# Turning the residual on VectorE, and three more up-projection units by [hi|lo] products, in a two-block transformer kernel

## What is computed

```python
    x = x + merged @ w_o
    h2 = rmsnorm(x, g_ffn)
    a, b = jnp.split(h2 @ w_up, 2, axis=-1)          # D_FF = 2816
    a = causal_dwconv3(a, ffn_conv_w, ffn_conv_b)
    x = x + (jax.nn.silu(a) * b) @ w_down
```

## Time and profile before

| | us |
|---|---|
| median of 3 runs (800.58 to 800.98) | 800.76 |
| the profiled execution, its own time | 800.36 |
| its span, first to last instruction | 798.5 |

### The profile page before, as it was taken

The page is one execution under the profiler, slowest core; times in us unless marked ns, Lnnn a source line. Parts: engine busy times, 40 slices in busy tenths (PEclk is TensorE's granted clock), DMA queues, the critical chain, the costliest instruction groups (busy, mean ns, idle before and its releaser), DMA issues.

```text
span 798.5 us, 11719 instructions
## 1 busy us (share of the span) xinstructions
PE 788.4 (99%) x4648; PEld 692.1 (87%) x4648; DVE 637.5 (80%) x943; ACT 445.1 (56%) x613; POOL 32.1 (4%) x32
## 2 busy tenths in 40 slices
PE   7899999999999999999999999999999999999998
PEld 7899778889999888888888887888899988888887
DVE  4998999997888997776887898755877777777775
ACT  7848677636556345454876655654436545545451
POOL 2000000000000000000000000000000121111210
PEclk9999999999999999999999999999999999999999
DMA  9997948964636875554354746544544555465411
GB/s 354 418 419 259 355 165 310 391 242 159 215 137 237 318 258 210 207 201 169 125 192 158 263 158 243 180 158 163 206 137 137 207 212 204 158 210 212 167 44 53
DMA packets 25909, 171.96 MB, mean 215 GB/s; under 512 B 2944, under 2 KB 3456, under 8 KB 5888
## 3 DMA queue, kind: packets, MB, share of 16 engines
q1 hardware_dynamic: 25712, 171.21, 58.2%
q10 hardware_dynamic: 144, 0.01, 0.0%
HBM read 170.16 MB, written 1.05 MB: 214 GB/s over the span
## 4 chain that ended last, share of the span: by engine, by line
PE 92%; DVE 5%; ACT 1%; DMA 1%; issue 1%; SPq 0%
PE ps L1763 57%; PE ps L1798 18%; PE ps L1805 9%; PE ps L1859 1%; DVE wlo L1102 1%; PE ps L2039 1%; DMA raw<-in_w_mem_kv 1%; PE ps L2072 1%; PE ps L2010 1%; PE ps L2011 1%; DVE wlo L1097 1%; ACT whi L530 1%; DVE side_x L1068 0%; PE ps L2154 0%; PE ps L2019 0%
## 5 line engine op out<-in xcount | busy, mean ns | idle before, releaser
L1102 DVE TENSOR_TENSOR wlo<-raw,whi 128x2048 fp32r<-128x2048 f32 (+1 forms) x130 | 287.2, 2215 | 62.2 <-ACT whi L530 57.8
L530 ACT ACTIVATE whi<-raw 128x2048 fp32r<-128x2048 f32 (+2 forms) x144 | 251.2, 1756 | 100.2 <-PE ps L1798 42.5
L1763 PE MATMUL ps<-whi,h_two 128*128 128x512 f32 x352 | 110.7, 396 | 0.0
L1763 PE MATMUL ps<-h_two,whi 128*128 128x256 f32 x544 | 99.5, 285 | 1.8 <-DVE wlo L1097 1.6
L1763 PEld LDWEIGHTS ps<-h_two,whi 128*128 128x128 f32 x544 | 84.7, 191 | 2.8 <-DVE wlo L1097 1.8
L1798 PE MATMUL ps<-h_two,whi 128*128 128x512 f32 x336 | 80.4, 390 | 0.0
L1763 PE MATMUL ps<-h_two,wlo 128*128 128x256 f32 x272 | 76.9, 283 | 0.0
L1763 PEld LDWEIGHTS ps<-whi,h_two 128*128 128x128 f32 x352 | 64.8, 188 | 13.3 <-issue 0.7
L1798 PEld LDWEIGHTS ps<-h_two,whi 128*128 128x128 f32 x336 | 62.1, 188 | 12.3
L1763 PE MATMUL ps<-whi,fhi 128*128 128x512 f32 (+1 forms) x178 | 69.0, 388 | 0.0
L1763 PE MATMUL ps<-whi,flo 128*128 128x512 f32 (+1 forms) x178 | 68.9, 387 | 0.0
(11 more groups left out here) (272 smaller groups left out, 1358.8 us busy)
## 6 DMA issues: line engine op xcount, KB each, us to landing
raw<-in_w_up SPq DMA_DIRECT2D x44, 1024.0 KB, 4.8
raw<-in_w_in SPq DMA_DIRECT2D x43, 1024.0 KB, 4.8
raw<-in_w_down SPq DMA_DIRECT2D x22, 1024.0 KB, 4.8
raw<-in_w_ada SPq DMA_DIRECT2D x14, 1024.0 KB, 5.2
raw<-in_branches SPq DMA_DIRECT2D x10, 1024.0 KB, 4.9
raw<-in_w_out SPq DMA_DIRECT2D x4, 1024.0 KB, 7.0
raw<-in_w_o SPq DMA_DIRECT2D x4, 1024.0 KB, 4.8
raw<-in_w_mem_kv SPq DMA_DIRECT2D x3, 1024.0 KB, 11.0
```

The source lines that it names most:

```text
L530: return nc.scalar.activation(dst, src, func, **kw)
L1102: V.tensor_tensor(wlo[:, w % SPLIT, c:UNIT], raw[:, slot, c:UNIT], f32(whi[:, w % SPLIT, c:UNIT]), ALU.subtract).then_inc(raw_done, 1)
L1763: ins = mm(out_, l, r, start=start and i == 0, stop=stop and i == 2, **kw)
```

## The change

Three things, all in the feed-forward of the second block:

1. g0, a1 and g1 become paired. g0 uses banks 4,5, a1 banks 6,7 (free now until d0), g1 banks 2,3. Each gets its ACT copy of the upper half and one more DVE addition. g0's unit waits for `x5_ready` >= 4 as do a1 and g1; the second half of d0 (banks 6,7) waits for `a_ready1` >= 2, that is, until DVE has read a1 out.
2. The 16 transposes on TensorE and ACT's two copies into `x_rows` are gone, and d0's wait for them.
3. DVE turns the residual by 32 `transpose` instructions. Each takes 32 partitions of `x` by 8 x 32 elements (eight square blocks of 32x32) to 32 partitions of `x_rows`. Four of them stand behind `split_low` in each slot of a_j, j = 2 to 9, ahead of the `split_low` and `convolve` of g_j.

```diff
-FIRST_PAIRED = (4, 2)
-PAIRED_A, PAIRED_G = ((0, 1), (0, 1)), ((2, 3), (2, 3))
+ROW_TURNS = 32
+FIRST_PAIRED = {"a": (4, 1), "g": (4, 0)}
+PAIRED_BANKS = {"a": ((0, 1), (0, 1)), "g": ((2, 3), (2, 3))}
+EARLY_BANKS = {("g", 0): (4, 5), ("a", 1): (6, 7)}
...
 # ScalarE
                 def gate_low(j, it=0):
-                    if paired(f, j):
-                        act.wait_ge(gemm_done, it * BODY + (w0 + 3 * j + 1))
-                        act.wait_ge(sem(f"glu_done{f}"), it * STEPS + j)
-                        copy(g_low[:, :, :], half_of(PAIRED_G[f], 1)).then_inc(sem(f"g_low{f}"), 1)
+                    if paired(f, "g", j):
+                        act.wait_ge(gemm_done, it * BODY + (w0 + (3 * j if j else 1) + 1))
+                        if j:
+                            act.wait_ge(sem(f"glu_done{f}"), it * STEPS + j)
+                        copy(g_low[:, :, :], half_of(paired_banks(f, "g", j), 1)).then_inc(sem(f"g_low{f}"), 1)
...
-                    if f == 1 and c == 2:
-                        act.wait_ge(sem("turned_in"), 9)
-                        for tt in range(NT):
-                            copy(x_rows[:, tt, :], ps[:, 4 + 2 * tt:6 + 2 * tt, :].rearrange("p a b -> p (a b)"))\
-                                .then_inc(sem("rows_ready"), 1)
...
 # VectorE
+                def turn_residual(n):
+                    tt, a, b = n // 16, n // 4 % 4, n % 4
+                    if n == 0:
+                        dve.wait_ge(sem("turned_in"), 8)
+                        dve.wait_ge(sem("x5_ready"), 4)
+                    rows = x_rows[32 * b:32 * b + 32, tt, :].rearrange("p (k c) -> p k c", k=KT)[:, :, 32 * a:32 * a + 32]
+                    V.transpose(rows, x[32 * a:32 * a + 32, :, P * tt + 32 * b:P * tt + 32 * b + 32]).then_inc(sem("rows_ready"), 1)
+
                 def slot(c, kind, j, it=0):
                     before_last = c == 3 * FJ - 2
                     if not before_last and not (f == 0 and c in (0, 3 * FJ - 1)):
                         split_low(w0 + c + AHEAD, it)
+                    if f and kind == "a":
+                        for n in range(4 * max(j - 2, 0), min(4 * max(j - 1, 0), ROW_TURNS)):
+                            turn_residual(n)
...
 # TensorE
-                    if paired(f, j):
-                        pe.wait_ge(sem(f"a_ready{f}" if kind == "a" else f"glu_done{f}"), it * STEPS + j)
-                        paired_channels(w, PAIRED_A[f] if kind == "a" else PAIRED_G[f], (h_two, g_two)[f], kind == "g")
+                    if paired(f, kind, j):
+                        if f and j < 2:
+                            pe.wait_ge(sem("x5_ready"), 4)
+                        else:
+                            pe.wait_ge(sem(f"a_ready{f}" if kind == "a" else f"glu_done{f}"), it * STEPS + j)
+                        paired_channels(w, paired_banks(f, kind, j), (h_two, g_two)[f], kind == "g")
+                        if f and c == 1:
+                            broadcast("ffn2")
+                        if f and c == 2:
+                            pe.wait_ge(sem("spread_r_ready"), 2)
                         return
...
-                    if f and c == 1:
-                        broadcast("ffn2")
-                        pe.wait_ge(sem("x5_ready"), 4)
-                        for tt in range(NT):
-                            for k in range(KT):
-                                at = P * (k % 4)
-                                ins = nc.tensor.transpose(ps[:, 4 + 2 * tt + k // 4, at:at + P], x[:, k, P * tt:P * tt + P],
-                                                          ident[:, :])
-                        ins.then_inc(sem("turned_in"), 1)
...
 # down
-                    if f and j == 0:
-                        pe.wait_ge(sem("rows_ready"), 2 * NT + 4)
                     for tt, half in ((0, 0), (0, 1), (1, 0), (1, 1)) if f else ROW_ORDER:
                         closing = last and (tt, half) == (1, 1)
+                        if f and j == 0 and tt == 1:
+                            pe.wait_ge(sem("a_ready1"), 2)
```

More of the change, by code:

```diff
@@ L332, in gate_pair, with paired, paired_banks @@
             return p // 2, slice(512 * (p % 2), 512 * (p % 2) + 512)
-        def paired(f, j):
-            return j >= FIRST_PAIRED[f]
+        def paired(f, kind, j):
+            return j >= FIRST_PAIRED[kind][f]
+        def paired_banks(f, kind, j):
+            return EARLY_BANKS.get((kind, j), PAIRED_BANKS[kind][f]) if f else PAIRED_BANKS[kind][f]
         def half_of(banks, low):
@@ L872, in pad_a @@
                 def pad_a(c, j, b, it=0):
-                    if paired(f, j):
+                    if paired(f, "a", j):
                         act.wait_ge(gemm_done, it * BODY + (w0 + c + 1))
                         act.wait_ge(sem(f"a_ready{f}"), it * STEPS + j)
-                        copy(a_low[:, :, :], half_of(PAIRED_A[f], 1)).then_inc(sem(A_LOW[f]), 1)
+                        copy(a_low[:, :, :], half_of(paired_banks(f, "a", j), 1)).then_inc(sem(A_LOW[f]), 1)
                         return
@@ L1498, in convolve @@
                     V.tensor_copy(cw[:, b, :, :], table[:, :, bass.ds(it * 2 * STEPS + 2 * j, 2)]).then_inc(conv_step, 1)
-                    if paired(f, j):
-                        first = FIRST_PAIRED[f]
+                    if paired(f, "a", j):
+                        first = FIRST_PAIRED["a"][f]
                         inner = fa[:, b, :, 2:S + 2]
                         dve.wait_ge(sem(A_LOW[f]), it * STEPS + (j + 1 - first))
-                        ins = V.tensor_tensor(inner, half_of(PAIRED_A[f], 0), a_low[:, :, :], ALU.add)
+                        ins = V.tensor_tensor(inner, half_of(paired_banks(f, "a", j), 0), a_low[:, :, :], ALU.add)
                         if f:
@@ L1548, in gate_it @@
                         ins.then_inc(sem("glu_done0"), 1)
-                    elif paired(f, j):
-                        n = it * STEPS + (j + 1 - FIRST_PAIRED[f])
+                    elif paired(f, "g", j):
+                        n = it * STEPS + (j + 1 - FIRST_PAIRED["g"][f])
                         dve.wait_ge(sem(f"g_low{f}"), n)
-                        V.tensor_tensor(pair(fp[:, b, :]), half_of(PAIRED_G[f], 0), g_low[:, :, :], ALU.add)\
+                        V.tensor_tensor(pair(fp[:, b, :]), half_of(paired_banks(f, "g", j), 0), g_low[:, :, :], ALU.add)\
                             .then_inc(sem(f"g_summed{f}"), 1)
@@ L1607, in add_halves @@
                 for i, b in enumerate(unit_banks(w)):
-                    dve.wait_ge(sem("low_copied"), FJ - FIRST_PAIRED[0] + 2 * (w - PAIRED_IN2) + i + 1)
+                    dve.wait_ge(sem("low_copied"), FJ - FIRST_PAIRED["a"][0] + 2 * (w - PAIRED_IN2) + i + 1)
                     V.tensor_tensor(low_tile(k, i), low_tile(k, i), ps[:, b, 0:S], ALU.add).then_inc(emptied["dve"], 1)
@@ L1738, in _ @@
             dve.wait_ge(gemm_done, FF[1] + 3 * FJ - 1)
-            dve.wait_ge(sem("rows_ready"), 2 * NT + 4)
+            dve.wait_ge(sem("rows_ready"), NT + 4 + ROW_TURNS)
             link(V.tensor_tensor(x_rows[:, 1, 512:1024], x_rows[:, 1, 512:1024], ps[:, 7, :], ALU.add))
@@ L2238, in up @@
                         channels(w, i, 256, *h, KT, last=i == 1, bank=bank)
-                    if f and c == 1:
-                        broadcast("ffn2")
-                        pe.wait_ge(sem("x5_ready"), 4)
-                        for tt in range(NT):
-                            for k in range(KT):
-                                at = P * (k % 4)
-                                ins = nc.tensor.transpose(ps[:, 4 + 2 * tt + k // 4, at:at + P], x[:, k, P * tt:P * tt + P],
-                                                          ident[:, :])
-                        ins.then_inc(sem("turned_in"), 1)
-                    if f and c == 2:
-                        pe.wait_ge(sem("spread_r_ready"), 2)
                 def down(c, j):
```

## The result

The changed kernel takes **812.02 us** (median of 4 runs, 811.48 to 812.4) against 800.87 us: a ratio of 1.0139, 95% interval 1.0121 to 1.0156. It is slower, as forecast, but by 11.2 us where 5.0 were forecast, and outside the range. The profiled execution has a span of 810.2 us (before 798.5).

A forecast was written before the change was run, and what follows sets the result against it. TensorE, 99% busy, was taken as the bound until transposes lengthen VectorE's chain from 15.74 to 17.10 us a round; d10 then starts at 784.28 + 8T = 795.16, +5.0 us, so 805.7 us. Range 801.0 to 809.5, its own 803.5 to 809.3.

The forecast's parts named there:

- a chain through VectorE: Second feed-forward: convolution, SiLU, POOL's product, gate, fhi, whi, splits; with transposes 17.10 us a round, over TensorE's 16.55.
- L = 15.74: Chain's need in us a round without transposes: 11.32 from cw copy to the split in a's slot, plus two splits of 2.21.
- C_1: Start of the cw copy ahead of convolution 1 in the second feed-forward; forecast at 635.92 us, before 637.02.
- d0's wait: TensorE, before writing d0's second half, waits about 1.2 us until a1 is read out; leaves 1.1 of 2.33 us saved.
- t = 0.34 us, T = 4t = 1.36: Distance between starts of VectorE transposes, and the time four add to the chain in each round, C_1 to C_9.
- The upper bound of 0.45: Largest t, in us, if each transpose waits for the one ahead, read from four operations taking 1.80 us.
- All behind d10 is unchanged.: End of the kernel: d10 starts 5.0 us later, at 795.16 against 790.20, and what follows takes as long as before.
- C_10: Start of the cw copy ahead of convolution 10, the chain's last; forecast near 786 us, before 780.59.
- The chain didn't keep up: Rival 1, second feed-forward: the chain keeps up, kernel not slower, if t is 0.185 us or less; 18%.
- rival 2: VectorE transposes cost more than one cycle an element: t = 0.61 us, d10 +13.6, 814.4 us; 8%.
- Rival 3: The chain has give: POOL's product could shorten; at 0.5 us a round the slip is +1 us, 801.8; 4%.
- The 1.1 us given as left after d0: Most that rival 1 can give, if transposes cost almost nothing: 799.7 us; up to 2.3 us, 798.4, without d0's wait.

The follow-up runs named there:

- no_turns: Changed kernel without the VectorE transposes, residual left out of the sum, rows filled with zeros by GpSimd; 0.9993 of the kernel before.
- half_turns: Changed kernel with every second transpose left out, two in each slot of a_j, the other blocks zero; 1.0040 of the kernel before.
- wide_turns: Changed kernel with 16 transposes of 32 x 512 in place of 32 of 256 elements, two in a slot; 1.0118 of the kernel before.
- gaps_early: Changed kernel with all transposes moved into VectorE's waits and a1 read out ahead of the split; 798.69 us, 0.9979 of the kernel before.
- one_quadrant: Changed kernel with all 32 transposes reading and writing the first 32 partitions only, most of the residual left out; 1.0090 of the kernel before.

## Why the prediction was right and wrong

- **That a chain through VectorE sets the pace once the transposes are in it: right.** The 11.32 us stand in the new profile, L = 15.74 in no_turns' first rounds (15.73, 15.72), half_turns came out at the round forecast from them, and taking the transposes out of the chain took the loss away.
- **The head: right.** C_1 was forecast 19.83 us behind the statistics and is 19.90 (636.14 - 616.24). d0's wait is 1.2 us. TensorE gets to d0 17.38 us behind the statistics after 19.66 before, 2.28 saved where 2.33 were forecast. The first gate that it waits for is g4's ("0.94" at each g_j from 680.4 on).
- **The step that failed first: "Where nothing is waited for, the next starts before the end ... I take t = 0.34 us, T = 4t = 1.36."** The two TENSOR_SCALARs it was read from both work on all 128 partitions. Each transpose of the change writes other partitions than the one ahead, waits for its end, and so starts 0.465 us behind it. The split behind the last is held in the same way, and so is the first transpose of a slot in six slots of eight. T is 1.95 us on average (1.85 in the two slots that begin at n = 0 and 16, 1.98 in six), eight rounds give 8 x 0.59 = 4.7 us more. The duration was guessed well (422 ns by the nearest row, 435 measured, 444 by the estimate from the Trainium skill's 311 ns, "VectorE: DVE Perf Modes", The three transpose paths); the overlap was not. The upper bound of 0.45 was itself read too low: four TENSOR_TENSORs of 422 ns in 1.80 us start (1.80 - 0.42) / 3 = 0.46 us apart, the transposes' distance, and 1.80 / 4 gives less.
- **The second: "All behind d10 is unchanged."** It wasn't: the waits ahead of d10 were taken as inside the sum, but not that TensorE, idle for 2.34 us, is then granted 1.2 GHz for 3.38 us. That is 1.7 us in the profiled execution. With 0.07 at the head and 0.11 between C_10 and d10 this closes the account: 4.96 + 4.7 + 0.18 + 1.71 = 11.55.
- **The rivals.** The chain didn't keep up, since a transpose takes 1.04 ns an element (wide_turns), not half of that. At t = 0.465 instead of 0.61 the runs also rule out the dearer transpose of rival 2. Rival 3: the chain had no give, 11.32 us before and after. The 1.1 us given as left after d0, if transposes cost nothing, is 0.8 (no_turns); the 2.3 with d0's wait gone is 2.27 (gaps_early), but it came from moving the transposes and the read-out, not from cheaper ones.
- **The range** ended at t = 0.45 and an unchanged end. The clock's 1.7 us alone would have stayed within it (807.4); the transposes' 4.7 alone pass it by 0.9 (810.4).

## What to carry to other kernels

When work goes to an engine that is 80% busy, find the chain through it that returns to the bounding engine, and its slack in one round (0.81 us here, none in rounds where the chain is already late): work inside the chain is paid in full over that slack, and work in the chain's own waits costs nothing as long as it fits (0.9 us in waits of 1.35 and 1.11). Price back-to-back instructions by rows that switch partitions as yours do. And where a bounding engine will newly stand idle for microseconds, price what comes behind the wait at the lower clock too.

## What the runs showed of the hardware that I had not expected

- These VectorE instructions overlap only where they start on the same 32 partitions as the one ahead: the first transpose then starts 2.20 us behind the start of a split of 2.29 us, otherwise 2.32. Transposes start 0.335 us apart instead of 0.465, and their own records are shorter too, 400 ns on average in one_quadrant against 435.
- After 2.35 us of idle time TensorE's clock falls to 1.2 GHz about 1 us after work has begun again (at once in wide_turns' profile, whose first matmul took 0.76 us), for 3.4 us in the changed kernel's profile, in two of three executions of such kernels. The waits of 0.94 us at the gates and of 1.2 us in d0 did not lower it (granted clock 1.00 through 620 to 780 us).
